# The order of GpSimd's gathers: the down row of pick n+1 is issued ahead of the up row of pick n

## The reference

```python
def block(args):                        # 128 tokens at a time, two blocks
    xb, ib, gb = args
    u = expert_down[ib]                 # (128 tokens, 8, 16, 2048)
    act = gelu(einsum('td,thkd->thk', xb, u))
    vv = expert_up[ib]
    return einsum('thk,thkd->td', gb * act, vv)
```

## Time and profile before

| | us |
|---|---|
| median of 3 runs | 3289.77 |
| lowest, highest | 3283.38, 3291.4 |
| profiled execution | 3288.06 |
| its span | 3286.1 |
| first gather issued | 531.85 |
| last sum of a pick done on VectorE | 2388.8 |

### The profile page before, as it was taken

The page is one execution under the profiler, slowest core; times in us unless marked ns, Lnnn a source line. Parts: engine busy times, 40 slices in busy tenths (PEclk is TensorE's granted clock), DMA queues, the critical chain, the costliest instruction groups (busy, mean ns, idle before and its releaser), DMA issues.

```text
span 3286.1 us, 23968 instructions
## 1 busy us (share of the span) xinstructions
PE 2937.9 (89%) x8013; PEld 1298.8 (40%) x8013; DVE 1237.3 (38%) x1897; ACT 545.0 (17%) x1292; POOL 706.7 (22%) x599
## 2 busy tenths in 40 slices
PE   8999998799898989897687887887799999999999
PEld 4444443344344434343333333333344433333344
DVE  1101005535344443345755756544532132322220
ACT  1111001112121110112213211221222111000010
POOL 1000002423233223323433444333400000000000
PEclk9999999999999999998888988898899999999999
DMA  9878887999999999999999999999977759999972
GB/s 353 304 278 288 301 305 295 417 412 408 410 367 416 421 422 421 421 422 417 407 419 377 411 419 418 419 419 419 415 259 259 261 221 422 422 422 422 422 300 77
DMA packets 268081, 1206.79 MB, mean 367 GB/s; under 512 B 16656, under 2 KB 19280, under 8 KB 164688
## 3 DMA queue, kind: packets, MB, share of 16 engines
q1 hardware_dynamic: 193600, 668.09, 52.7%
q0 software_dynamic: 74384, 537.49, 39.7%
HBM read 1203.41 MB, written 2.10 MB: 367 GB/s over the span
## 4 chain that ended last, share of the span: by engine, by line
PE 48%; DMA 38%; DVE 5%; issue 3%; DVEq 2%; ACT 1%; SPq 1%; POOL 0%; ACTq 0%; POOLq 0%
DMA W<-in_peer_expert_down,big 24%; PE bank L949 14%; DMA W<-in_w_expert_up 8%; PE bank L1501 7%; PE bank L939 5%; PE bank L1111 5%; PE bank L1608 4%; DMA W<-in_w_in 3%; PE bank L1666 3%; PE bank L1016 3%; DMA XT<-in_peer_expert_up,big 2%; DVE W L2567 2%; DVEq L2417 2%; PE bank L1592 1%; DMA W<-in_w_peer_query 1%
## 5 line engine op out<-in xcount | busy, mean ns | idle before, releaser
L2567 DVE CUSTOM_DVE_ANT_0 W<-W,big 128x2048 f32<-128x2048 f32 x256 | 586.1, 2291 | 692.5 <-DMA W<-in_peer_expert_down,big 691.3
L877 POOL DMA_INDIRECT W<-in_peer_expert_down,big x256 | 349.9, 1367 | 1220.5 <-DVE small L2567 637.5
L1501 PE MATMUL bank<-XT,big 128*128 128x512 f32 x488 | 301.5, 775 | 211.5 <-ACT big L1949 169.8
L949 PE MATMUL bank<-W,XT 128*128 128x512 f32 x704 | 309.5, 598 | 2.6 <-DMA W<-in_w_peer_query 2.6
L1501 PEld LDWEIGHTS bank<-XT,big 128*128 128x128 f32 x488 | 119.4, 254 | 380.7 <-issue 249.8
L1501 PE MATMUL bank<-XS,big 128*128 128x512 f32 x536 | 246.2, 603 | 21.5 <-ACT big L1949 19.4
L1501 PE MATMUL bank<-W,big 128*128 128x512 f32 x512 | 237.3, 607 | 30.8 <-ACT big L1949 25.1
L1941 ACT ACTIVATE small<-small 128x1 f32<-128x1 f32 x256 | 51.8, 202 | 1224.8 <-DVE small L2567 1210.3
L1608 PE MATMUL bank<-W,XS 128*64 128x512 f32 x1024 | 225.3, 593 | 14.2 <-DMA W<-in_w_expert_up 11.6
L1111 PE MATMUL bank<-W,XT 128*128 128x512 f32 x480 | 218.8, 606 | 21.2 <-DMA W<-in_w_in 19.0
L939 PE MATMUL bank<-W,XT 128*128 128x512 f32 x480 | 211.0, 597 | 3.6 <-DMA W<-in_w_in 3.6
(11 more groups left out here) (383 smaller groups left out, 2684.0 us busy)
## 6 DMA issues: line engine op xcount, KB each, us to landing
W<-in_w_in SPq DMA_DIRECT2D x66, 2048.0 KB, 7.9
W<-in_w_in SPq DMA_DIRECT2D x132, 1024.0 KB, 11.9
W<-in_w_expert_gate SPq DMA_DIRECT2D x68, 1024.0 KB, 15.0
W<-in_w_expert_up SPq DMA_DIRECT2D x68, 1024.0 KB, 17.0
big<-in_w_expert_down SPq DMA_DIRECT2D x32, 2048.0 KB, 12.6
W<-in_w_out SPq DMA_DIRECT2D x16, 2048.0 KB, 8.0
W<-in_w_out SPq DMA_DIRECT2D x32, 1024.0 KB, 11.6
W<-in_w_peer_query SPq DMA_DIRECT2D x28, 1024.0 KB, 10.9
```

What stands on the lines that cost most here:

```text
L877: pool.indirect_dma_start(down_row(n), None, down_t, row).then_inc(down_in[n % DOWN_ROWS], 16)
L949: mm = pe.matmul(out, lhs(k), slot(i)[:, k, :], start=first and k == 0, stop=last and k == ks - 1)
L1501: mm = pe.matmul(bank[4 * (n // P) + c][:, :], DIAG[:, m % 4, :], up_row(n)[:, c * CH:(c + 1) * CH], start=n % P == 0, stop=n % P == P - 2)
L2567: dve.tensor_tensor_reduce(out=down_row(n), in0=down_row(n), in1=HN[n // P], scale=1.0, scalar=0.0, op0=ALU.mult, op1=ALU.add, accum_out=d ...
```

## The change

The loop of POOL over the picks is split into two functions with the same instructions and the same waits. The down row of pick 0 is issued first; then, for every n, the down row of pick n + 1 and after it the up row of pick n. The last up row, of pick 255, stands alone at the end.

```diff
-            for n in range(PICKS):
+            def rows_at(n):
+                return bass.IndirectOffsetOnAxis(idx_all[:, n // P, n % P:n % P + 1], 0)
+
+            def gather_down(n):
                 if n % BATCH == 0:
                     pool.wait_ge(idx_ready, n // BATCH + 1)
-                row = bass.IndirectOffsetOnAxis(idx_all[:, n // P, n % P:n % P + 1], 0)
                 if n >= DOWN_ROWS:
                     pool.wait_ge(dotted, n - DOWN_ROWS + 1)
                 pool.sem_inc(gathers, 1)
-                pool.indirect_dma_start(down_row(n), None, down_t, row).then_inc(down_in[n % DOWN_ROWS], 16)
+                pool.indirect_dma_start(down_row(n), None, down_t, rows_at(n)).then_inc(down_in[n % DOWN_ROWS], 16)
+
+            def gather_up(n):
                 b, earlier, _ = UP_ROWS[n]
...
                 pool.sem_inc(gathers, 1)
-                pool.indirect_dma_start(up_row(n), None, up_t, row).then_inc(up_in[b], 16)
+                pool.indirect_dma_start(up_row(n), None, up_t, rows_at(n)).then_inc(up_in[b], 16)
+
+            gather_down(0)
+            for n in range(PICKS):
+                if n + 1 < PICKS:
+                    gather_down(n + 1)
+                gather_up(n)
```

## The result

The changed kernel took 3295.84 us, median of 9 runs (3294.03 to 3300.83); the kernel before, beside it, 3289.5 (3279.24 to 3292.28, 9 runs). The ratio is 1.0026, with an interval of 1.0017 to 1.0035: 6.3 us by the medians, on the side of a loss and inside what was forecast as no change.

The account below looks back on a forecast made before the run. It took the transfers to bound the gather stretch; 2.5 + 1.3 + 1.0 + 1.5 - 2.2 = +4.1 us on the profiled 3288.06 gave 3292.2, with 1.7 for the median 3293.9, forecast as 3293, range 3279 to 3308.

Parts of the forecast that it names:

- The two gap terms, 2.5 and 1.3: Transfer gaps at 978 to 986 and 752: the held up row leaves the queue one row less, +2.5 and +1.3 us.
- the zeros beside them: Gap at 902 to 914, with TensorE the bound (at most 2.5 us), and the saturated start: no cost at either.
- R: Gaps where VectorE stands: the held up row leaves one row less in the draining queue, as the prediction had reckoned.
- The turn of the tile, 1.0 (0 to 2.5): Change of token tile: U(128) lands 4.9 us later, 2.4 of it slack, so VectorE stalls +1.0 us.
- the convolution, 1.5 (0 to 6.6): Convolution at 1741.95: ScalarE's copies end 6.56 us later, at 1743.49, so it starts +1.5 us later.
- rule of turns between queues: Engines alternate queues packet by packet: a row costs 5.0 us, gap terms 7.6 instead of 3.8, time 3297.
- The wait of 13.62 in the earlier trace: Wait ending at 1797.82, on a chain starting with a dot product: 0, or 2.5 us if the 1800 gap deepens.
- B: Rival: TensorE's extra lag opens new VectorE stops, five places of 3.6 us, 18 us, giving 3308; chance 0.27.
- The end, -2.2: Last sum starts on the landing of U(255), its weight long ready: -2.2 us, between -2.5 and 0.
- Rival A: Rival: held down rows matter more, earlier filling recovers half the gaps' 20.7 us and the tail, 3278; chance 0.18.
- C: Rival: the transfer bound hides everything and signs cancel, 3290 within 1 or 2 us; chance 0.18 together with D.
- D: Rival: POOL finds D(n+1) blocked, the lead is order and not time, 3290 to 3293; chance 0.18 together with C.

Follow-up runs that it names:

- TensorE's shift: TensorE adds pick n - 1 instead of pick n in tick n: with the new order 0.9993 of the kernel before, with the old order 0.9981.
- the second tile alone: Old order for picks 0 to 127, new order for picks 128 to 255, against the kernel before: 3287.2 us, ratio 1.0005.
- A lead of two: Down rows issued two picks ahead, D(n+2) before U(n), instead of one, against the kernel before: 3360.91 us, ratio 1.0230.

## Why the prediction came out

**The mechanism.** The steps on the streams held. The down stream kept its time and the up stream came a pick later: at pick 64 the dot product starts 1.3 us later than before and the up row's issue 9.2, at pick 80 it is 1.2 and 9.8. The rate in undisturbed windows is the same; TensorE's waits for up rows grew and those for the diagonal shrank. "Costs arise where the queue runs dry" held too. The size of 6 us comes for the most part from other places than the sum said.

**The two gap terms, 2.5 and 1.3, and the zeros beside them: the step that failed.** The sum charged the held up row at the gaps around 978 and 752. The timeline of POOL after (start, length, line, tiles, count, idle before and releaser), with the rows that answer to the earlier trace rows:

```profile
981.70 2.59 POOL L881 DMA_INDIRECT W<-in_peer_expert_down,big  x1 [10.05 <-DVE small L2580]
984.59 2.72 POOL L893 DMA_INDIRECT XS<-in_peer_expert_up,big  x1 [0.30 <-issue]
```

The up row (984.59) is held behind the same wait of 10.05 us, as said, and the gap is no larger: 984 to 992 at 351 GB/s misses 1.3 us, 978 to 986 missed 1.8, and the bytes from 960 to 1040 miss 3.0 for 3.2. This term is nil. The one at 752 does show in the transfers, with about the size that was given to it: the windows from 736 to 772 have 13.94 MB for 14.38, which misses 2.9 us for 1.8.

The mechanism of these terms opened the largest new gap elsewhere, at 672, where the kernel before had none and the sum nothing. The timeline of POOL, before and then after:

```profile
674.75 1.32 POOL L886 DMA_INDIRECT XT<-in_peer_expert_up,big  x1 [18.95 <-PE bank L1501]
679.01 2.95 POOL L877 DMA_INDIRECT W<-in_peer_expert_down,big  x1 [2.94 <-DVE small L2567]
```

```profile
681.56 2.95 POOL L881 DMA_INDIRECT W<-in_peer_expert_down,big  x1 [25.41 <-DVE small L2580]
684.82 0.94 POOL L893 DMA_INDIRECT XT<-in_peer_expert_up,big  x1 [0.30 <-issue]
```

VectorE stands there for a result of the other engines, 17.39 us before and 26.73 after. The up row used to go out as soon as TensorE had freed its buffer; now it stands behind the down row and goes out 10.1 us later, and nothing is issued for 25.41 us. By their bytes the windows from 660 to 704 miss 4.2 us, for 1.2 before; the other kernels with the lead in the first tile and TensorE's part unchanged miss 3.4 to 4.5, those with the lead elsewhere 1.2 and 1.6. Whether the gaps at 672 and 752 cost time isn't shown: TensorE's sums are 2.5 us later than before at 673 and at 719, and 1.9 at 777, so its own lag doesn't grow over them. R isn't excluded as a part of the loss of the first 56 picks.

TensorE's chain, on which the 5.8 us at its last matmul lie, was late from places that got a zero: "at 902 to 914 TensorE is the bound, and a later up row is hidden behind it", and "at the start nothing". The first eight sum matmuls of TensorE, before and then after:

```profile
542.51 5.41 PE L1501 MATMUL bank<-W,big 128*128 128x512 f32 x8 [12.33 <-ACT big L1949]
```

```profile
544.21 5.64 PE L1514 MATMUL bank<-W,big 128*128 128x512 f32 x8 [13.30 <-DMA W<-in_peer_expert_up,big]
```

The up row of pick 0 goes out 2.0 us later, behind a second down row, and TensorE starts on its landing, 1.7 us later than it did on the diagonal. TensorE is indeed the bound at 902, but what it works off there depends on when the waits before it ended. The chain of waits, start and length in us, before and then after:

```profile
603.31 18.33 DMA XT<-in_peer_expert_up,big
...
621.68 5.09 PE bank L1501 x8
...
840.91 16.17 DMA W<-in_w_in
...
857.12 3.70 PE bank L1111 x8
...
869.88 21.93 DMA W<-in_w_in
...
898.38 3.43 PE bank L1501 x8
```

```profile
606.32 18.85 DMA XT<-in_peer_expert_up,big
...
625.21 6.12 PE bank L1514 x8
...
844.22 20.29 DMA W<-in_w_in
...
864.55 5.40 PE bank L1124 x8
...
879.00 19.80 DMA W<-in_w_in
...
904.24 3.43 PE bank L1514 x8
```

A weight load of the query that follows goes out 1.9 us later and takes 31.28 us instead of 30.20, and so the up row of pick 12, whose buffer TensorE has to free, goes out 3.0 us later and its matmuls start 3.5 later. From there the chain is for the most part a ring: a load of weights lands, TensorE works, frees the place, and the next load goes out. By 844 it is 3.3 behind. Then a load takes 20.29 instead of 16.17, which puts it 7.4 behind; part comes back, and 904.24 against 898.38 are 5.9. The picks catch up later, as seen above, the weights don't. That matches 5.8 at the last matmul on these weights, and the 6.3 of the medians. How the lag gets into the ring (a tick that waits ahead of its matmuls on weights) is read from this chain and agrees with TensorE's shift; it isn't proved by them. That the longer load was due to an up row in flight beside it was only argued, and other executions speak against reading much into it: with the shift the load at 839.37 takes 20.30, and that kernel is no slower than before. In place of 3.8 the first tile's term measures 5.9 at this point of the chain and 6.7 in missing transfers at 1000.

**The turn of the tile, 1.0 (0 to 2.5), and the convolution, 1.5 (0 to 6.6).** Timeline after, answering to the earlier trace rows:

```profile
1608.08 6.18 PE L1514 MATMUL bank<-XT,big 128*128 128x512 f32 x8 [8.76 <-DMA XT<-in_peer_expert_up,big]
...
1618.17 2.48 DVE L2110 TENSOR_TENSOR XT<-bank,GT 128x512 f32<-128x512 f32 x4 [3.11 <-PE bank L968]
...
1747.58 2.35 DVE L2431 SCALAR_TENSOR_TENSOR H<-XS,small,H 128x2048 f32<-128x2048 f32 x1 [1.75 <-DMA XS<-in_peer_expert_up,big]
...
1749.89 0.09 DVE L2503 MEMSET big<- 128x32 f32 x1
```

At the turn TensorE begins 11.3 us later than before, 5.1 of which the dot product of pick 128 is late already: the lag is 6.2, not 4.9, and VectorE stalls 3.1 us, above the bound of 2.5. The convolution starts 7.9 later with the dot product of its pick 6.3 later: +1.6, the predicted size, but the wait is VectorE's for its own up row, not for ScalarE's copies. Neither shows in the time: the second tile alone is at 1.0005 (0.9995 to 1.0015).

By the Trainium skill, DMA: Bandwidth & Descriptors, section Queues, rings and completion order, the descriptors of one ring start in ring order. No run here tests that by itself: of the lag of 11.3 us at the turn 9.5 are there when POOL issues the up row, so it is POOL's order and its waits that make it. The section's rule of turns between queues, by which the prediction's estimate would have been 3297, is nearer in number to the 3295.84 measured, but the larger of the two terms that it doubled is nil.

**The wait of 13.62 in the earlier trace rows, 0.** It answers as 11.76 us, ending at 1802.88: no cost, and B's count of such places isn't borne out here. Its sign, new windows under 350 GB/s at VectorE's waits, does appear once, at 672 (325 GB/s), but far from the 18 us that B reckoned. A lead of two comes near B, at +2.3%.

**The end, -2.2.** Wrong in sign in the trace. The last dot product before:

```profile
2383.45 2.29 DVE L2567 CUSTOM_DVE_ANT_0 W<-W,big 128x2048 f32<-128x2048 f32 x1 [2.64 <-DMA W<-in_peer_expert_down,big]
```

The last dot product and the last sum after, on VectorE, then the windows there (same columns as above):

```profile
2390.93 2.29 DVE L2580 CUSTOM_DVE_ANT_0 W<-W,big 128x2048 f32<-128x2048 f32 x1 [2.69 <-DMA W<-in_peer_expert_down,big]
...
2395.98 2.35 DVE L2431 SCALAR_TENSOR_TENSOR H<-XS,small,H 128x2048 f32<-128x2048 f32 x1 [2.75 <-DMA XS<-in_peer_expert_up,big]
```

```profile
2392.00:2393.00 1.00, 0.83 (x2) 0.00 (x0) 1.00 (x1) 0.00 (x0) 0.00 (x0) 1.00 0.51 213
2393.00:2394.00 1.00, 0.58 (x2) 0.34 (x3) 0.23 (x2) 0.50 (x2) 0.00 (x0) 1.00 0.14 57
2394.00:2395.00 1.00, 1.00 (x4) 0.52 (x3) 0.00 (x0) 0.00 (x0) 0.00 (x0) 1.00 0.06 25
2395.25:2396.00 0.75, 0.75 (x3) 0.37 (x2) 0.02 (x1) 0.00 (x0) 0.00 (x0) 1.00 0.00 0
```

The sum begins 5.05 us behind the last dot product; before it was 3.00. It does begin within 1 us of the last landing (2395.83), as the prediction said, but that landing comes later than it reckoned. It turned a mean share of 0.04 in four microseconds into an end of the transfers at 2384.2. A mean share gives the time that is missing, not when the last packet goes: the transfers thin out over some three microseconds, in which few of the 16 engines still work, and in windows of a quarter of a microsecond the last ones of before lie between 2385.00 and 2385.25, those of after between 2395.00 and 2395.25. Of the two orders the last row to land is on the path in one and beside it in the other.

**Rival A** (the held down rows win, 3278) fell: VectorE's waits for down rows shrank by 139 us and nothing was won, and the rate in undisturbed windows stayed at 418 to 420 GB/s: the transfers, not the issue, set the rows' rate. C, that the signs cancel, falls narrowly, its 1 or 2 us being less than the 1.0017 that the interval starts at; D falls with the up rows, whose lag is one of time. So the sum was near by number only, which is luck: its 4.1 us were made of other terms than the one of about 6 that it had priced at nothing. From the last sum to the end the profile has 900.6 us for 897.1; 3.1 of the difference arise behind 2650, in the experts, where the change does nothing.

## What to carry to other kernels

When a load is put ahead of another on one issuing queue, ask for the one that is held not only who waits for it, but what else stands behind that wait in its consumer's program, and whether that work gives back places to a second stream of loads. Such a lag is paid back by moving the consumer a tick, not the issue; the consumer's buffer is then freed a tick later, and the queue that refills it must not carry the pacing load behind it. Here moving TensorE's use alone, without the new order, was worth 0.19%. A change that mends a loss must also be tried without the loss: only this control showed that the shift gains by itself.

## What was not expected of the hardware

The last row doesn't end at the rate of the stretch. The DMA share falls from 0.96 in the microsecond from 2391 to 0.51, 0.14 and 0.06 in the next three, the last packets go before 2395.25, and the row counts as landed 0.6 us later, at 2395.83.

Two stalls of TensorE of the same length can be followed by different clocks. After 1.99 us of idling, at 656.24 in the kernel before, eight matmuls took 3.70 us at a granted clock of 1.00 (2.4 GHz); after 1.98 us, at 852.48 in the new order with TensorE's shift, they took 5.40 us, with 0.72 granted in the 6 us from 852, which is part of them at 1.2 GHz. TensorE had worked without a break for more than 10 us ahead of either stall. So a stall of TensorE can cost 1.7 us more than its length.

And 420 GB/s in a stretch doesn't mean that neither stream falls behind: from 1000 to 1500 after, the rate is nearly whole, while the weights fall 2.5 MB behind.
